# Expert blocks of two mixture-of-experts layers: sixteen uniform blocks plus three spares, or blocks by rank of expert with pairs of small ones

## The chip, the cores and the metric

One core of one Trainium2 chip runs the whole program. The metric is device time in microseconds, the median of several executions. TensorE is called PE below, VectorE DVE, ScalarE ACT, GpSimd POOL and SyncE SP; PEld is PE's loading of the stationary operand.

## The reference

The model is a first block (delta rule, dilated attention, a product-key expert layer) and two further layers. Each of these two ends in a mixture layer over T = 256 tokens, width D = 1024, with 16 experts of hidden width 512; every token picks 2 experts:

```python
weight = p_grp_sel * top_p / jnp.sum(top_p, axis=-1, keepdims=True)
expert = grp[:, None] * MOE_EXPERTS_PER_GROUP + top_i
...
def expert_block(args):
    xblk, e = args                     # 128 rows
    return (jax.nn.silu(xblk @ w1[e]) * (xblk @ w3[e])) @ w2[e]
```

So 512 rows in all are spread over 16 experts, each with w1 and w3 (1024x512) and w2 (512x1024), 2 MB each in float32: 96 MB of weights a layer. Only the two mixture layers are changed.

## The kernel before

`moe_blocks` runs one mixture layer after a normalisation stage that also makes the router's logits. DVE finds each token's two experts, PE counts how many rows each expert has, and DVE works out block and place of each row. An expert that has over 128 rows gets a second block from three spare ones, so there are NB = 19 blocks of 128 rows: sixteen by expert number, three whose expert is read from `moe_overflow_expert` at run time. POOL gathers a block's rows from DRAM (`moe_block_rows`, indirect DMA), and stores each block's result; at the end it gathers the rows back for every token, and the last two blocks are combined by PE from SBUF (`combine`).

A product of a block is made exact enough by splitting: ACT copies the weights to a rounded type (`high`, L2464), DVE subtracts that from the original (`low`, L144), and three products, low by high, high by low and high by high (L150, L151, L152), are summed in PSUM. A 2 MB weight matrix is split in two halves of 128x2048. The same is done to the block's transposed rows (ACT L2479, DVE L144) and to the hidden values (L2509, L144). A block has 8 x 3 products for w1, as many for w3 and 4 x 2 x 3 for w2: 72 products of 128x512, and 12 transposes (8 of rows, L2381; 4 of hidden values, L2390).

The weights come through a ring of three slots of 2 MB, loaded by SP: load m waits until both halves of slot m-3 are split, and does not wait for PE. `weight_parts` has room for two split matrices. As experts are taken in their own order, the plan of loads is fixed, and the stage before the mixture layer has already filled all three slots. The order on PE in block i is: w1 of i, transposes of the rows of i+1, w3 of i, w2 of i-1, transposes of the hidden values of i.

Each engine works through its instructions in the order written. A wait holds up everything that stands behind it on that engine.

Of the kernel before, what the change touches and what calls it, by code (L numbers as in the profile page):

```python
# [77 lines left out]
def shape_constants():  # L78
# [17 lines left out]
    cst[:, C_PLACE:C_PLACE + P] = p + 1  # L96
# [58 lines left out]
class WeightStream:  # L155
# [3 lines left out]
    def __init__(self, nc, ctx):  # L159
        self.ring = ctx.enter_context(nc.sbuf_tensor("weight_ring", [P, SLOTS, SLOTW], F32))  # L160
        self.loaded = [ctx.enter_context(nc.semaphore(f"weights_loaded_{i}")) for i in range(SLOTS)]
        self.used = ctx.enter_context(nc.semaphore("weights_used"))
        self.plan = []
        self.issued = 0
        self.taken = 0
# [5 lines left out]
    def add_block(self, src, k, width):  # L171

        self.plan.append((src.rearrange("p (k n) -> p k n", k=k), k, width))

    def add_later(self, k, width):

        self.plan.append((None, k, width))
# [4 lines left out]
    def load(self, sp, upto):  # L182

        for n in range(self.issued, min(upto, len(self.plan))):
# [2010 lines left out]
OVER = 3  # L2195
NB = NE + OVER


def slot_w1(i):

    return 3 * i - 1 if i else 0


def slot_w3(i):

    return 3 * i if i else 1


def slot_w2(i):

    return 3 * i + 4 if i < NB - 1 else 3 * NB - 1


def plan_moe(S, layer):

    w1, w3, w2 = (S.dram[f"moe_{n}_2"][layer] for n in ("w1", "w3", "w2"))

    def one(src, i, k, width):  # L2220
        if i < NE:
            S.w.add_block(src[i], k, width)
        else:
            S.w.add_later(k, width)
    for i in range(NB):
        one(w1, i, KD, FF)
        one(w3, i, KD, FF)
        if i:
            one(w2, i - 1, FF // P, D)
    one(w2, NB - 1, FF // P, D)  # L2230
# [14 lines left out]
def moe_blocks(S, layer, lg, p8, rows_of_x, rows_of_y):  # L2245
# [4 lines left out]
    EARLY, MIX_AT = NB - 2, 4  # L2250
    with Stage(S, "moe") as st:
# [8 lines left out]
        late = st.sb("pick_early_late", [P, 3, 2 * NT])  # L2260
        token_mix = st.sb("token_mix", [P, 4, P])
        place_mix = st.sb("place_mix", [P, 4, P])
# [7 lines left out]
        less = st.sb("expert_before", [P, NE, NE])  # L2270
        ov = st.sb("overflows", [P, NE])
        oc = st.sb("overflow_rank", [P, NE])
        wide_ov = st.sb("overflow_before", [P, NE, NE])
        at_hot = st.sb("at_pick", [P, 2 * NT, NE])
        pos = st.sb("pick_place", [P, 2 * NT])
        rank = st.sb("pick_rank", [P, 2 * NT])
        ov4 = st.sb("pick_over", [P, 2 * NT])
        blk = st.sb("pick_block", [P, 2 * NT])
        yrow = st.sb("pick_row_f", [P, 2 * NT])
        yix = st.sb("pick_row", [P, 2 * NT], U32)  # L2280
# [3 lines left out]
        ox = st.sb("overflow_hot", [P, OVER, NE])  # L2284
        oe = st.sb("overflow_expert_f", [P, OVER])
        oei = st.sb("overflow_expert", [P, OVER], U32)

        wp = st.sb("weight_parts", [P, 2, 2, SLOTW])
        xg = st.sb("block_rows", [P, 2, D])
        xt = st.sb("block_x_parts", [P, 2, 2, KD, P])  # L2290
        g = st.sb("hidden", [P, FF])
        gt = st.sb("hidden_parts", [P, 2, 2, FF // P, P])
        y = st.sb("block_out", [P, 2, D])
        xr = st.sb("first_pick_rows", [P, NT, D])
        pick_rows = (xr, S.hT[:, :, :].rearrange("p k t -> p (k t)").rearrange("p (a d) -> p a d", a=NT))
        places = st.sb("places", [P, C_ALL - C_PLACE])
        block_number = places[:, P + 4:P + 4 + NB].rearrange("p (o n) -> p o n", o=1)
        place = places[:, 0:P].rearrange("p (o n) -> p o n", o=1)
        token = places[:, P:P + 2 * NT].rearrange("p (q o) -> p q o", o=1)

        chain, shifted, exped, hot_made, counted, placed, indexed, experts_known = (st.sem(n) for n in (
            "chain", "shifted", "exped", "hot_made", "counted", "placed", "indexed", "experts_known"))
        mixed, mix_turned, mix_moved, early_gated, last_gated, combined = (st.sem(n) for n in (
            "mixes_made", "mixes_turned", "mixes_moved", "early_gated", "last_gated", "combined"))
        back_turned, back_moved, places_in = (st.sem(n) for n in ("x_turned_back", "x_rows_moved", "places_in"))
        x_stored = [st.sem(f"x_rows_stored{a}") for a in range(NT)]
        high_made, split_made, spent = (st.sem(n) for n in ("weights_high", "weights_split", "weights_spent"))
# [7 lines left out]
        n0, N = S.w.taken, 3 * NB  # L2315
        w1, w3, w2 = (S.dram[f"moe_{n}_2"][layer] for n in ("w1", "w3", "w2"))
        ident = S.cst[:, C_ID:C_ID + P]
        H1, H3, XT, GT, Y, RB = 0, 1, 2, 4, 5, 7
        BACK = (0, 1, 5, 6)
        half = lambda m, h: wp[:, m % 2, :, h * SLOTW // 2:(h + 1) * SLOTW // 2]  # L2320
        raw_half = lambda m, h: S.w.ring[:, (n0 + m) % SLOTS, h * SLOTW // 2:(h + 1) * SLOTW // 2]
# [3 lines left out]
        iota = lambda n: S.cst[:, C_IOTA:C_IOTA + n].rearrange("p (o n) -> p o n", o=1).to_broadcast([P, NT, n])  # L2325
        with nc.Block() as block:
            @block.sync
            def _(sp):
                sp.dma_start(places[:, :], S.dram["cst"][:, C_PLACE:C_ALL]).then_inc(places_in, 16)
                S.w.load(sp, n0 + SLOTS)  # L2330

                def load(m, src):

                    _, k, width = S.w.plan[n0 + m]
                    sp.wait_ge(split_made, 2 * (m - SLOTS) + 2)
                    sp.dma_start(S.w.view(n0 + m, k, width), src).then_inc(S.w.loaded[(n0 + m) % SLOTS], 16)
                for m in range(SLOTS, slot_w1(NE)):
                    load(m, S.w.plan[n0 + m][0])
# [16 lines left out]
            def _(pe):  # L2355
# [19 lines left out]
                def turn_x(i):  # L2375
                    pe.wait_ge(gathered[i % 2], 16 * (i // 2 + 1))
                    if i:
                        pe.wait_ge(xt_high, i)
                        pe.wait_ge(xt_low, i)
# [664 lines left out]
```

## Time and profile before

| | |
|---|---|
| three runs | 2562.29, 2553.57, 2560.84 us, median 2560.84 |
| span of the profiled execution | 2554.6 us |
| median less this span | 6.2 us; the record has no other time of the profiled execution |
| mean granted TensorE clock | 0.958 of full speed |
| first mixture layer, first product to last addition | 1540.28 to 1904.54 us of the span |
| second mixture layer | from about 2188 us to the end |
| weight loads of the two layers | 114 of 2 MB |

A row of the timeline gives start, duration, engine, line and operation, with its output and inputs. The profiler's matmul durations hold a fixed tail, so the distance between two starts is the cost of one in a run of them. A plain float32 matmul leaves two records, one of float32r leaves one.

### The profile page before, as it was taken

The page shows a single profiled execution, that of the slowest core. Times are in us where ns is not written, and L with a number is a line of the kernel's source. Part 1 is how long each engine was busy: PE and PEld are TensorE (multiplying, and loading weights), DVE is VectorE, ACT ScalarE, POOL GpSimd, SP SyncE. Part 2 cuts the span into 40 slices and gives each one's busy share as a digit, 9 for nine tenths or more (in the row PEclk, how much of TensorE's full clock was granted, in tenths as well). Part 3 has the DMA queues.
Part 4 walks back from the last instruction along what each step waited for, and adds up shares of the span by engine and source line. Part 5 has one row for each costly group of instructions (what it writes and reads, how often), then busy time and mean ns, then how long its engine had stood idle before and what let it go on. Part 6 is the DMA issues. An engine that isn't in the chain of part 4 may idle for free. (4 is left out here: it accounts for less than half of the span.)

```text
span 2554.6 us, 29254 instructions
## 1 busy us (share of the span) xinstructions
PE 2229.2 (87%) x11200; PEld 1600.9 (63%) x11200; DVE 1765.0 (69%) x2586; ACT 848.7 (33%) x1127; POOL 474.8 (19%) x418
## 2 busy tenths in 40 slices
PE   7788998888987777777898989999989778999998
PEld 6688886564532222222477957788869575678886
DVE  5355643458888886555654667898887575788988
ACT  1311101111111110000102325777750331677785
POOL 1032000113443434344120011000010021101001
PEclk9789999999999999999987999999999978999999
DMA  5720663439999999999562028999984504799996
GB/s 204 270 100 2 231 198 132 169 110 399 408 421 421 421 422 422 421 417 422 221 179 99 1 94 299 373 409 411 413 307 165 198 2 179 268 379 403 411 412 263
DMA packets 147335, 707.36 MB, mean 277 GB/s; under 512 B 16039, under 2 KB 20799, under 8 KB 99675
## 3 DMA queue, kind: packets, MB, share of 16 engines
q1 hardware_dynamic: 96604, 391.84, 40.2%
q0 software_dynamic: 48640, 310.47, 29.6%
q10 hardware_dynamic: 1952, 3.18, 0.4%
q8 instruction: 90, 1.47, 0.2%
q14 instruction: 49, 0.40, 0.0%
HBM read 684.40 MB, written 21.05 MB: 276 GB/s over the span
## 5 line engine op out<-in xcount | busy, mean ns | idle before, releaser
L144 DVE TENSOR_TENSOR moe_weight_parts<-weight_ring,moe_weight_parts 128x2048 fp32r<-128x2048 f32 x228 | 512.2, 2288 | 57.5 <-ACT moe_weight_parts L2464 57.2
L1608 PE MATMUL psum<-peer_uv_rows,peer_weight_diagonal 128*128 128x512 f32 x932 | 453.2, 615 | 107.5 <-DVE peer_weight_diagonal L1734 107.2
L2464 ACT ACTIVATE moe_weight_parts<-weight_ring 128x2048 fp32r<-128x2048 f32 x228 | 423.4, 1910 | 45.3 <-DMA weight_ring<-moe_w 40.7
L1608 PEld LDWEIGHTS psum<-peer_uv_rows,peer_weight_diagonal 128*128 128x128 f32 x932 | 161.9, 190 | 389.5 <-DVE peer_weight_diagonal L1734 263.3
L1741 DVE SCALAR_TENSOR_TENSOR peer_uv_rows<-peer_uv_rows,peer_x 128x1024 f32<-128x1024 f32 x233 | 285.6, 1226 | 142.5 <-DMA peer_uv_rows<-peer_uv,peer_index 140.3
L1562 POOL DMA_INDIRECT peer_uv_rows<-peer_uv,peer_index x233 | 242.2, 1040 | 385.8 <-PE psum L1608 330.6
L150 PE MATMUL psum<-moe_weight_parts,moe_block_x_parts 128*128 128x512 f32 x608 | 247.1, 406 | 7.1 <-DVE moe_weight_parts L144 5.6
L152 PE MATMUL psum<-moe_weight_parts,moe_block_x_parts 128*128 128x512 f32 x608 | 239.8, 394 | 0.0
L151 PE MATMUL psum<-moe_weight_parts,moe_block_x_parts 128*128 128x512 f32 x608 | 239.7, 394 | 0.0
L1641 ACT ACTIVATE peer_gelu<-peer_dots 128x1 f32<-128x1 f32 x256 | 51.5, 202 | 548.1 <-DVE peer_uv_rows L1741 497.1
L144 POOL TENSOR_TENSOR project_x_parts<-h_t,project_x_parts 128x1024 fp32r<-128x1024 f32 x16 | 52.7, 3312 | 533.1 <-ACT project_x_parts L630 533.1
L144 DVE TENSOR_TENSOR project_weight_parts<-weight_ring,project_weight_parts 128x2048 fp32r<-128x2048 f32 (+2 forms) x60 | 146.0, 2433 | 2.1
L150 PEld LDWEIGHTS psum<-moe_weight_parts,moe_block_x_parts 128*128 128x128 f32 x608 | 115.9, 191 | 32.5 <-issue 10.5
L152 PEld LDWEIGHTS psum<-moe_weight_parts,moe_block_x_parts 128*128 128x128 f32 x608 | 115.8, 191 | 25.5
L151 PEld LDWEIGHTS psum<-moe_weight_parts,moe_block_x_parts 128*128 128x128 f32 x608 | 116.3, 191 | 22.1
L2522 POOL DMA_DIRECT2D moe_results<-moe_block_out x34 | 19.7, 580 | 585.8 <-ACT moe_block_out L2486 585.8
L150 PE MATMUL psum<-moe_weight_parts,moe_hidden_parts 128*128 128x512 f32 x304 | 122.0, 401 | 4.5 <-DVE moe_hidden_parts L144 4.5
L150 PE MATMUL psum<-project_weight_parts,project_x_parts 128*128 128x512 f32 (+2 forms) x320 | 123.8, 387 | 0.0
L151 PE MATMUL psum<-project_weight_parts,project_x_parts 128*128 128x512 f32 (+2 forms) x320 | 122.0, 381 | 0.0
L152 PE MATMUL psum<-project_weight_parts,project_x_parts 128*128 128x512 f32 (+2 forms) x320 | 122.0, 381 | 0.0
L152 PE MATMUL psum<-moe_weight_parts,moe_hidden_parts 128*128 128x512 f32 x304 | 119.3, 392 | 0.0
L151 PE MATMUL psum<-moe_weight_parts,moe_hidden_parts 128*128 128x512 f32 x304 | 119.0, 392 | 0.0
(543 smaller groups left out, 3835.0 us busy)
## 6 DMA issues: line engine op xcount, KB each, us to landing
weight_ring<-moe_w SPq DMA_DIRECT2D x114, 2048.0 KB, 10.6
weight_ring<-ada_w SPq DMA_DIRECT2D x24, 2048.0 KB, 9.5
weight_ring<-w_in SPq DMA_DIRECT2D x17, 2048.0 KB, 8.6
moe_results<-moe_block_out POOLq DMA_DIRECT2D x34, 512.0 KB, 10.9
weight_ring<-hgrn_w_in SPq DMA_DIRECT2D x8, 2048.0 KB, 10.7
weight_ring<-nsa_w_in SPq DMA_DIRECT2D x5, 2048.0 KB, 9.1
weight_ring<-peer_wq SPq DMA_DIRECT2D x4, 2048.0 KB, 10.2
weight_ring<-w_out SPq DMA_DIRECT2D x2, 2048.0 KB, 10.4
```

Source lines behind the costliest of these rows:

```text
L144: return eng.tensor_tensor(out.bitcast(F32R), x, high, ALU.subtract)
L150: nc.tensor.matmul(out, ll, rh, start=start, stop=False)
L151: nc.tensor.matmul(out, lh, rl, start=False, stop=False)
L152: return nc.tensor.matmul(out, lh, rh, start=False, stop=stop)
L1562: nc.gpsimd.indirect_dma_start(buffer(t), None, S.dram["peer_uv"], bass.IndirectOffsetOnAxis(ap=experts[:, t:t + 1], axis=0)).then_inc(row ...
L1608: last = nc.tensor.matmul(S.ps[:, 2 * a + c, :], diag[:, t % 4, :], v_rows(t)[:, c * BANK:(c + 1) * BANK], start=(i == 0), stop=(i == PICK ...
L1641: act.activation(act_of[:, t:t + 1], dots[:, t:t + 1], ACT.Gelu_apprx_tanh).then_inc(geared, 1)
L1741: nc.vector.scalar_tensor_tensor(u_rows(t), u_rows(t), 1.0, x2[:, t // PICKS, :], ALU.mult, ALU.mult, accum_out=dots[:, t:t + 1]).then_inc ...
L2464: act.activation(half(m, h)[:, 0, :].bitcast(F32R), raw_half(m, h), ACT.Copy).then_inc(high_made, 1)
L2522: pool.dma_start(rows_of_y[i * P:(i + 1) * P, :], y[:, i % 2, :]).then_inc(y_stored[i % 2], 16)
```

## The change

Experts are ranked by how many rows they have. There are 15 blocks (jobs) in 12 units: ranks 0 to 2 have two blocks each that share one read of the weights ("doubled"), ranks 3 to 7 one block each ("single"), and ranks 8 to 15 are taken in pairs: one block holds 64 rows of one expert and 64 of the other. All weights are read once, 48 loads a layer in place of 57. A pair is not split: its products are plain float32, two for each step, one for each half of 64 columns of the stationary operand, and each writes its own 64 partitions of PSUM.

All loads now depend on the ranking, so none is issued before DVE has made it (`experts_known`), and the stage before does not load ahead (`hold`). The ring has a fourth slot. A slot of a split matrix is released when it is split, a slot of a pair only when PE has used it (`plain_spent`). The split halves have four places, as before. The first nine jobs run in three groups, each a doubled unit and a pair. Only the last job is combined from SBUF. Ranking adds some ten small DVE operations before the first gather. Core of the diff:

```diff
-OVER = 3
-NB = NE + OVER
+NB = 15
+RING = SLOTS + 1
+HALVES = 4
+    unit = [((0,), (0, 1)), ((8, 9), (11,)), ((1,), (2, 3)), ((10, 11), (12,)), ((2,), (4, 5)), ((12, 13), (13,)),
+            ((3,), (6,)), ((4,), (7,)), ((5,), (8,)), ((6,), (9,)), ((7,), (10,)), ((14, 15), (14,))]
+def phase_order():
+    for g in range(3):
+        for w in "132":
+            order += [(2 * g, w), (2 * g + 1, w)]
+    order += [(6, "1"), (6, "3")]
+    for u in range(6, LAST):
+        order += [(u + 1, "1"), (u, "2"), (u + 1, "3")]
+    return order + [(LAST, "2")]
 def plan_moe(S, layer):
+    S.w.hold()
+        def released(eng, m):
+            u, w, _ = SLOT_OF[m]
+            if PAIR[u]:
+                eng.wait_ge(plain_spent, PLAIN_AT[u, w] + 1)
+            else:
+                eng.wait_ge(split_made, 2 * SPLIT_AT[u, w] + 2)
 @@ SP @@
+                sp.wait_ge(experts_known, 1)
+                for m, (u, w, side) in enumerate(SLOT_OF):
...
+                    if m >= RING:
+                        released(sp, m - RING)
...
+                    sp.dma_start(slot(m).rearrange("p (k n) -> p k n", k=steps[w]), src).then_inc(loaded[m % RING], 16)
 @@ PE @@
+                def up_pair(u, w, first, end):
...
+                        for side in range(2):
+                            half = slice(64 * side, 64 * side + 64)
+                            last = nc.tensor.matmul(S.ps[half, LANES[2][w == "3"], :], xp[:, k, half], weights[side][:, k, :],
+                                                    start=(k == 0), stop=(k == KD - 1))
+                for gr in range(3):
...
+                    else:
+                        up(a, "1", 0)
+                    turn_x(jq, 0)
+                    up(a, "1", 1)
+                    turn_x(jq, 1)
+                    up_pair(q, "1", 0, KD)
+                    up(a, "3", 0)
+                    up(a, "3", 1)
+                    up_pair(q, "3", 0, 2)
+                    turn_x(jq + 1, 0)
+                    up_pair(q, "3", 2, 4)
+                    turn_hidden(ja)
+                    up_pair(q, "3", 4, 6)
+                    turn_x(jq + 1, 1)
+                    up_pair(q, "3", 6, KD)
+                    turn_hidden(jb)
+                    down(a, 0)
+                    turn_hidden(jq)
+                    down(a, 1)
+                    turn_x(jq + 2, 0)
+                    down_pair(q, 0, 2)
+                    turn_x(jq + 2, 1)
+                    down_pair(q, 2, 4)
+                for u in range(6, LAST - 1):
+                    up(u + 1, "1", 0)
+                    turn_hidden(i)
+                    up(u + 1, "1", 1)
+                    turn_x(i + 2, 0)
+                    down(u, 0)
+                    turn_x(i + 2, 1)
+                    down(u, 1)
+                    up(u + 1, "3", 0)
+                    up(u + 1, "3", 1)
 @@ ACT, in a group (s = 3 * gr) @@
+                    high(2 * s + 2)
+                    x_high(jq, 0)
+                    high(2 * s + 3)
+                    x_high(jq, 1)
+                    silu(ja)
+                    silu(jb)
+                    silu(jq)
+                    high(2 * s + 4)
+                    high(2 * s + 5)
+                    x_high(jq + 1, 0)
+                    hidden_high(ja)
+                    x_high(jq + 1, 1)
+                    hidden_high(jb)
+                    high(2 * s + 6)
+                    hidden_high(jq)
+                    high(2 * s + 7)
+                    out(ja)
+                    out(jb)
+                    x_high(jq + 2, 0)
+                    x_high(jq + 2, 1)
+                    out(jq)
 @@ DVE, in a group @@
+                    low(2 * s + 2)
+                    low(2 * s + 3)
+                    low(2 * s + 4)
+                    low(2 * s + 5)
+                    gate(ja)
+                    gate(jb)
+                    x_low(jq + 1, 0)
+                    hidden_low(ja)
+                    x_low(jq + 1, 1)
+                    hidden_low(jb)
+                    gate(jq)
+                    low(2 * s + 6)
+                    low(2 * s + 7)
+                    x_low(jq + 2, 0)
+                    x_low(jq + 2, 1)
```

`high(n)` waits for the load of the matrix that half n belongs to. `turn_x(i, r)` transposes half r of a job's rows and waits until ACT has taken the half before it (`xt_high`). `turn_hidden` waits for `gate`. ja, jb and jq are the two jobs of the doubled unit and that of the pair.

## Rows read from the trace of the kernel before

**Rows 1.** The page: span, and busy time of PE with its share.

```profile
span 2554.6 us, 29254 instructions
...
PE 2229.2 (87%) x11200; PEld 1600.9 (63%) x11200; DVE 1765.0 (69%) x2586; ACT 848.7 (33%) x1127; POOL 474.8 (19%) x418
```

**Rows 2.** Both mixture layers as stretches: busy by engine, clock, DMA share, GB/s.

```profile
1540.00:1897.00 357.00, 346.57 (x1594) 283.06 (x1595) 308.96 (x201) 260.48 (x188) 33.54 (x38) 0.98 0.94 376
...
2187.00:2540.00 353.00, 344.04 (x1594) 280.68 (x1594) 308.26 (x199) 261.15 (x188) 33.88 (x38) 0.99 0.94 377
```

**Rows 3.** PE's timeline in steady blocks: start, duration, operation.

```profile
1690.33 0.60 PE L2390 MATMUL psum<-constants,moe_hidden 128*128 128x128 f32 x4
...
1696.26 1.03 PE L2381 MATMUL psum<-constants,moe_block_rows 128*128 128x128 f32 x8
...
1708.19 0.60 PE L2390 MATMUL psum<-constants,moe_hidden 128*128 128x128 f32 x4
...
1800.05 0.39 PE L150 MATMUL psum<-moe_weight_parts,moe_block_x_parts 128*128 128x512 f32 x1
...
1800.96 0.39 PE L151 MATMUL psum<-moe_weight_parts,moe_block_x_parts 128*128 128x512 f32 x1
```

**Rows 4.** Groups by form, 1540 to 1897: count, busy us, mean ns, idle before.

```profile
L144 DVE TENSOR_TENSOR moe_weight_parts<-weight_ring,moe_weight_parts 128x2048 fp32r<-128x2048 f32 x112 | 251.6, 2288 | 29.2 <-ACT moe_weight_parts L2464 29.0
L2464 ACT ACTIVATE moe_weight_parts<-weight_ring 128x2048 fp32r<-128x2048 f32 x110 | 204.4, 1910 | 25.1 <-DMA weight_ring<-moe_w 22.3 <-PE psum L152 2.7
...
L2486 ACT ACTIVATE moe_block_out<-psum 128x1024 f32<-128x1024 f32 x18 | 18.5, 1028 | 28.7 <-PE psum L152 28.7
...
L144 DVE TENSOR_TENSOR moe_hidden_parts<-psum,moe_hidden_parts 128x512 fp32r<-128x512 f32 x19 | 13.1, 690 | 4.8 <-ACT moe_hidden_parts L2509 4.6
L2660 DVE TENSOR_TENSOR moe_hidden<-moe_hidden,psum 128x512 f32<-128x512 f32 x19 | 12.9, 681 | 3.2 <-PE psum L152 3.2
...
L2509 ACT ACTIVATE moe_hidden_parts<-psum 128x512 fp32r<-128x512 f32 x19 | 11.3, 592 | 2.3 <-PE psum L2390 2.3
```

**Rows 5.** PE's timeline: float32 products on four 32-column parts of the array.

```profile
87.77 1.95 PE L342 MATMUL psum<-weight_ring,cond 128*32 128x128 f32 x64
```

**Rows 6.** PE's timeline: two full float32 products of 512 columns.

```profile
802.58 1.98 PE L1608 MATMUL psum<-peer_uv_rows,peer_weight_diagonal 128*128 128x512 f32 x4 [0.50 <-DVE peer_weight_diagonal L1734]
```

**Rows 7.** Issue to landing: L2336; conditioning loads at 63.4; load at 1534.69; block gathers.

```profile
DMA to landing us min/median/max: 7.9/10.6/12.4
...
weight_ring<-ada_w SPq DMA_DIRECT2D x2, 2048.0 KB, 11.0
...
weight_ring<-moe_w SPq DMA_DIRECT2D x1, 2048.0 KB, 9.8
...
DMA to landing us min/median/max: 5.2/15.9/17.8
```

**Rows 8.** A stall of PE: timeline at 1634, and the stretch behind it.

```profile
1630.15 0.60 PE L2390 MATMUL psum<-constants,moe_hidden 128*128 128x128 f32 x4
...
1634.00 1.11 PE L2432 MATMUL psum<-constants,moe_token_mix 128*128 128x128 f32 x4 [3.26 <-DVE moe_token_mix L2643]
...
1637.00:1639.00 2.00, 2.00 (x6) 1.56 (x5) 1.35 (x1) 0.00 (x0) 0.00 (x0) 0.50 1.00 424
...
1642.68 1.04 PE L2381 MATMUL psum<-constants,moe_block_rows 128*128 128x128 f32 x8
```

**Rows 9.** Timeline at the first layer's start.

```profile
1524.59 0.18 DVE L2591 TENSOR_REDUCE moe_totals<-psum 128x16 f32<-128x32 f32 x1
...
1536.82 1.04 PE L2381 MATMUL psum<-constants,moe_block_rows 128*128 128x128 f32 x8
...
1540.28 0.47 PE L150 MATMUL psum<-moe_weight_parts,moe_block_x_parts 128*128 128x512 f32 x1 [0.70 <-issue]
```

**Rows 10.** Timeline at the first layer's end.

```profile
1896.25 7.03 PE L2422 MATMUL psum<-moe_block_out,moe_place_mix 128*128 128x512 f32 x16
...
1903.32 1.22 DVE L2704 TENSOR_TENSOR h<-h,psum 128x1024 f32<-128x1024 f32 x1 [0.42 <-PE psum L2422]
```

More of the change, by code:

```diff
@@ L163, in __init__ @@
         self.plan = []
+        self.holds = []
         self.issued = 0
@@ L182, in load @@
     def load(self, sp, upto):
-        for n in range(self.issued, min(upto, len(self.plan))):
+        for n in range(self.issued, min([upto, len(self.plan)] + self.holds[:1])):
             if n >= SLOTS:
@@ L2354, in _ @@
+                for j in range(SLOTS):
+                    m = N - RING + (j - N) % RING
+                    if m == SLOT_AT[LAST, "3", 1]:
+                        sp.wait_ge(added, NT)
+                    released(sp, m)
+                    if j == 0:
+                        S.w.holds.pop(0)
+                    S.w.load(sp, n0 + j + 1)
             @block.tensor
@@ new lines, in down_pair @@
+                def down_pair(u, first, end):
+                    i, = JOBS_OF[u]
+                    weights = raw(u, "2")
+                    pe.wait_ge(gt_high, i + 1)
+                    for f in range(first, end):
+                        for c in range(2):
+                            for side in range(2):
+                                half = slice(64 * side, 64 * side + 64)
+                                last = nc.tensor.matmul(S.ps[half, LANES[2][c], :], gp[:, f, half], weights[side][:, f, c * 512:(c + 1) * 512],
+                                                        start=(f == 0), stop=(f == FF // P - 1))
+                    if end == FF // P:
+                        last.then_inc(plain_spent, 1)
@@ new lines, in _ @@
+                up_pair(LAST, "1", 0, 4)
+                turn_hidden(LATE - 1)
+                up_pair(LAST, "1", 4, KD)
+                down(LAST - 1, 0)
+                down(LAST - 1, 1)
+                up_pair(LAST, "3", 0, KD)
+                pe.wait_ge(mixed, NT)
+                for a in range(NT):
+                    last = nc.tensor.transpose(S.ps[:, XB, a * P:(a + 1) * P], ohs[:, a, :], ident)
+                last.then_inc(mix_turned, 1)
+                turn_hidden(LATE)
+                down_pair(LAST, 0, FF // P)
@@ new lines, in _ @@
+                n = 2 * SPLIT_AT[6, "3"]
+                high(n)
+                high(n + 1)
+                high(n + 2)
+                silu(JOBS_OF[6][0])
+                high(n + 3)
+                high(n + 4)
+                high(n + 5)
+                n += 6
+                for u in range(6, LAST - 1):
+                    i, = JOBS_OF[u]
+                    hidden_high(i)
+                    for h in range(6):
+                        if n + h < 2 * len(SPLITS):
+                            high(n + h)
+                        if h == 0:
+                            x_high(i + 2, 0)
+                        if h == 1:
+                            silu(i + 1)
+                        if h == 2:
+                            x_high(i + 2, 1)
+                        if h == 3:
+                            out(i)
+                    n += 6
@@ new lines, in _ @@
+                n = 2 * SPLIT_AT[6, "3"]
+                for h in range(5):
+                    low(n + h)
+                gate(JOBS_OF[6][0])
+                low(n + 5)
+                n += 6
+                for u in range(6, LAST - 1):
+                    i, = JOBS_OF[u]
+                    hidden_low(i)
+                    for h in range(6):
+                        if n + h < 2 * len(SPLITS):
+                            low(n + h)
+                        if h == 0 and not PAIR[JOBS[i + 2][0]]:
+                            x_low(i + 2, 0)
+                        if h == 2 and not PAIR[JOBS[i + 2][0]]:
+                            x_low(i + 2, 1)
+                        if h == 4:
+                            gate(i + 1)
+                    n += 6
```

598 lines of the change are left out of this document (317 added, 281 removed).

## The prediction

> **What bounds the kernel now.** I read the page first, for the shares: PE is busy for 87% of 2554.6 us [rows 1]. That average says little of the two layers that change, so I next took them as stretches [rows 2]. PE is busy for 346.57 of 357 us and 344.04 of 353, at full clock, with the DMA engines at 0.94. Both limits are near. The timeline shows which one sets the pace: transposes of hidden values start at 1690.33 and 1708.19, a period of 17.86 us a block [rows 3]. Products follow each other by (1800.96 - 1800.05) / 4 = 0.227 us, so 72 of them are 16.3 us, and the 12 transposes take the other 1.5 us (0.13 each). PE never waits in such a block; it is the bound. The first layer runs from its first product at 1540.28 [rows 9] to its last addition, 1903.32 + 1.22 = 1904.5 [rows 10]: 364.3 us. Of this 19 x 17.87 = 339.5 are blocks and 24.8 are start, one stall and end.
>
> **The work that PE gets.** Eleven blocks stay split, 11 x 17.87. A pair has 16 + 8 steps, each of two float32 products of 512 columns on separate halves of the array. One such product at full width costs about (1.98 - 0.27) / 2 = 0.85 us, where 0.27 is the tail that a last record holds over its pitch [rows 6]. Do two halves run at once? The row that tells is the conditioning product: 64 records, which are 32 float32 products of 128 columns on four separate 32-column parts, in 1.95 us with the tail [rows 5]. One product of 128 columns is a quarter of 0.85, 0.213; 32 one after another would be 6.8 us, eight rounds of four at once are 1.7. So the parts run at once, and a pair's step costs 0.85, its 24 steps 20.5 us; one after another is the upper end, 41. On PE alone a group (two split blocks and a pair) is 6 x 5.44 + 20.5 + 36 transposes (4.7) = 57.8 us, for four blocks or 71.5 us before. That would be 13.7 won in each of three groups.
>
> The Trainium skill ("TensorE: Matmul & The Clock Gate", Measured speedup vs the span model) has 2.38 times for three column tiles, not three. At that efficiency a step would be 1.07 us by estimate, and the group 5.2 us dearer; the trace's four parts do not agree with it.
>
> **What the loads cost now.** Before, load m waited for a split, and three slots were full beforehand. Now a pair's slots come free only when PE has used them, and the ring is four deep. A group's nine loads are a1, q1, q1, a3, q3, q3, a2, q2, q2 (a the doubled unit, q the pair). Load m waits for m-4, so:
> - at the end of the pair's w1 phase the second q3 and a2 can start;
> - at the end of its w3 phase the second q2 and the next a1;
> - at the end of its w2 phase the second next q1 and the next a3.
>
> SP stands at each of these waits with all later loads behind it. The price of a restart: a lone 2 MB load lands 7.9 us after issue [rows 7]. The second adds at least 2.1 MB at the stretch's own pace: three loads and 1 MB of rows in 17.87 us is 7.34 MB, 411 GB/s, so 5.1 us. The ends for two are therefore 13.0 and, from the pair at 63.4, where the median 11.0 of both leaves 14.1 for the second and it was issued about 0.6 later, 14.7. I take 13.5, nearer to the MoE's rate. A load among gathers took 9.8 instead of 7.9 [rows 7]; rows of 0.5 MB cost 1.3 us each at that rate. At the group's end a gather and two stores are in flight, but the first microseconds of a load's latency cover most of it: 14.7 there. For the next a1 one gather counts half: 14.0.
>
> The Trainium skill ("DMA: Bandwidth & Descriptors", Anatomy of one DMA) gives 2.0 us + bytes / 436e3, by estimate 6.8 us for a lone load and 11.6 for two. By it a group would be 5.6 us shorter; the trace's minimum of 7.9 does not agree.
>
> **The chain through a group**, with ACT halves at 1.9, DVE halves at 2.29, moves of 512 columns at 0.6 on ACT and 0.69 on DVE, outputs at 1.03 [rows 4], all in written order:
> 1. From the end of the pair's w2 to a3's landing, 14.7. `high(2s+2)` 1.9, and only behind it `x_high(jq, 0)` 0.6, for which `turn_x(jq, 1)` on PE waits; 0.5 for it; then w1 of the pair, 8 x 0.85 = 6.8; 0.3 of gaps. 24.8 in all. PE had only 2 x 5.44 + 0.5 = 11.4 us of other work there and then idles about 6.
> 2. From there to a2's landing, 13.5. `high` 1.9, both `low` 4.6 (DVE has them ahead of `gate(ja)`), gate 0.7, `turn_hidden(ja)` 0.5, four pair steps 3.4, a transpose group 0.5, gaps 0.2: 11.8. Together 25.3. PE's own work up to `turn_hidden(ja)` is 10.9 + 3.4 + 0.5 after the first point; a2's chain is 20.7, so it idles some 6 us again.
> 3. From there to the next a1, 14.0. `high(2s+6)` 1.9, `hidden_high(jq)` 0.6, for which `down_pair` waits, `high(2s+7)` 1.9, two outputs 2.1, `x_high(jq+2, 0)` 0.6, the transposes 0.5, the last four steps 3.4, gaps 0.2: 11.2. Together 25.2. PE idles about 4 and then 1 us.
>
> The sum is 75.3 us, against 71.5 for the same four blocks now: loads, ACT's order and the pair make a ring of waits. The first group starts with four slots on order and takes about 73.7.
>
> **The clock.** In the stall at 1634 PE waited for 3.26 us, the granted clock was then 0.50 (1.2 GHz), and from the transposes at 1630.15 the next came at 1642.68 where 5.93 + 3.26 would have done [rows 3, 8]: 3.3 us lost, some 0.5 of it other transposes. So a stall of 3 us cost nearly its own length again. The three stalls of a group are as long or longer, and behind each stands pair work that the next loads wait for. I price each at 2.2 (ends 0 and 3.4), 6.5 a group: 81.8 us, 80 for the first.
>
> **Singles.** PE's 17.87 stays. ACT has 6 x 1.9 + 2 x 0.6 + 0.6 + 0.6 + 1.03 = 14.8 and DVE 6 x 2.29 + 4 x 0.69 = 16.5 us a block, both under it, and splits run two matrices ahead. The fourth and fifth load of this stretch start only at the last group's end, which costs about 5 us once, less what overlaps: up(6) to the end of iteration 9 is 88.4 us at full clock, 90.7 with one dip, for five blocks or 89.4 before.
>
> **Start.** `experts_known` comes seven small DVE operations (about 2.8 us) after the totals at 1524.59 [rows 9], 1527.4; with 1.5 for SP's register reads and 8 for the load, slot 0 is there at about 1537.5, split by 1541.7. The longer DVE sequence puts the first transposes 1.9 later than 1536.82. First product 1542.4, which is +2.1. The earlier stages lose nothing, they only no longer load ahead.
>
> **End.** The last pair's second w3 and both w2 loads start when its w1 is done: 7.9 + 5.2 + 5.2 + 1.2 of contention, so w2 starts 27 us after the unit does and ends at 33.9; the gathers of the results, behind `plain_spent`, land by 36 to 37, then DVE's row mixing, the gated output, the combination and the additions: 45.2 us, 48.2 with clock dips. Now the two blocks and the end cost 364.3 - 17 x 17.87 = 60.5, with the 16 us of early stalls in it.
>
> **Sum for a layer:** 2.1 + 80 + 2 x 81.8 + 90.7 + 48.2 = 384.6 against 364.3, +20.3. Two layers: +40.6 on a span of 2554.6, 2595. The median stood 6.2 above that span, so 2601 us, 1.6% slower.
>
> **The rivals.**
> - *The same waits at a lower price.* Loads of two in 13.0 us and no dip: a group is 72 and a layer 347.7 with a slightly shorter start, singles and end; -16.6 a layer, 2528 us. At 13.5 to 14.7 without a dip a layer is 2.1 + 73.7 + 150.6 + 88.4 + 45.2 = 360.0: -4.3 a layer, 2552 us, at the edge of what can be told. For it: the dip after 1634 hid partly behind other work; against: each stall here is longer. The point that decides is a group of 76 us: above it the layer loses. Chances 0.14 and 0.12.
> - *The loads don't hold anything up*, because they land before ACT needs them: PE's 57.8 a group, a layer of 303, 2439 us. For it: 48 loads and 15 blocks' rows (100.7 + 15.7 MB) are only 283 us of DMA at 411 GB/s. Against: a four-slot ring with slots freed by PE. Chance 0.12.
> - *The halves of a pair run one after another.* w1 +6.8, w3 +3.4 (the first four steps are hidden), w2 +5.5, over six groups 94 us, and about 31 in the two last units: 2726 us. [rows 5] speak against it. Chance 0.06.
> - The forecast: 0.56, its own range 2565 to 2640.
>
> **How the numbers follow.** About 0.3% (8 us) is what a measurement here tells from nothing. Faster takes the cheap waits and the unhindered loads, 0.26; same the 2552 case, 0.12; slower 0.62. The range leaves out 2439 and 2726 (0.18 together): 2520 to 2650.
>
> **What would show it.** PE idle for 4 to 6 us three times a group, before the pair's w1 (behind ACT's `x_high`), within its w3 (behind DVE's `gate`) and before its w2 (behind `hidden_high`), with ACT's `high` waiting for loads; load to landing near 8 to 14 us; a group of about 82 us; the clock at 0.5 behind the stalls; a pair's w1 phase of 6.8 us. I am wrong if the weights' landing is not what ACT waits for, if pair steps are not 0.85, or if the clock holds.

## The result, and the profile after

The changed kernel takes 2609.94 us (median of 4, from 2605.97 to 2616.59), the kernel before 2560.87 in the same comparison: a ratio of 1.0203 (95% interval 1.0182 to 1.0224), 2.0% slower. The forecast was 2601. The page and the two layers as stretches, over stretches of the same length as in [rows 1, 2] (busy us by engine, granted clock, DMA share, GB/s):

```profile
span 2608.5 us, 28034 instructions
...
PE 2174.5 (83%) x10700; PEld 1441.2 (55%) x10700; DVE 1435.0 (55%) x2420; ACT 584.6 (22%) x993; POOL 455.9 (17%) x402
```

```profile
1541.00:1898.00 357.00, 300.55 (x1288) 196.94 (x1288) 140.53 (x109) 133.59 (x121) 23.08 (x27) 0.91 0.75 302
2222.00:2575.00 353.00, 300.04 (x1290) 195.12 (x1290) 139.60 (x108) 133.16 (x121) 23.08 (x27) 0.91 0.75 303
```

DVE does less than half of what it did there, and PE's busy share, the DMA share and the clock all fell in the first layer: 0.84 for 0.97, 0.75 for 0.94, 0.91 for 0.98. With nothing near its limit, I looked for engines that wait for each other in turn. PE's timeline shows where (start, duration, operation, idle time before it and what ended it):

```profile
1545.04 1.94 PE L2433 MATMUL psum<-constants,h_t 128*128 128x128 f32 x8 [7.29 <-DMA h_t<-moe_tokens,moe_block_tokens]
...
1547.63 0.76 PE L150 MATMUL psum<-moe_weight_parts,moe_block_x_parts 128*128 128x512 f32 x1 [0.65 <-ACT moe_block_x_parts L2610]
...
1564.20 7.09 PE L2499 MATMUL psum<-weight_ring,moe_pair_x 128*64 128x512 f32 x32
...
1592.13 1.11 PE L2443 MATMUL psum<-constants,moe_hidden 128*128 128x128 f32 x4 [5.42 <-DVE moe_hidden L2772]
...
1616.39 0.79 PE L2513 MATMUL psum<-moe_weight_ring_end,moe_hidden 128*64 128x512 f32 x1 [4.93 <-ACT moe_hidden L2625]
...
1643.98 1.09 PE L2433 MATMUL psum<-constants,h_t 128*128 128x128 f32 x4 [6.47 <-issue]
...
1674.01 1.12 PE L2443 MATMUL psum<-constants,moe_hidden 128*128 128x128 f32 x4 [5.31 <-DVE moe_hidden L2772]
...
1697.44 3.41 PE L2513 MATMUL psum<-weight_ring,moe_hidden 128*64 128x512 f32 x10 [4.06 <-ACT moe_hidden L2625]
...
1723.77 1.09 PE L2433 MATMUL psum<-constants,h_t 128*128 128x128 f32 x4 [5.20 <-issue]
```

The first hidden transposes of each group (`turn_hidden(ja)`, L2443) start at 1592.13, 1674.01 and 1754.61: periods of 81.9 and 80.6 us. Each group has one stall within the pair's w3 and one ahead of its w2, and all but the first have one ahead of the pair's w1 (before `turn_x(jq, 1)`, put down to issue). What the engines that PE waits for were themselves waiting for is on ACT's timeline of two of these stalls, and on DVE's of the third:

```profile
1613.85 1.91 ACT L2596 ACTIVATE moe_weight_parts<-weight_ring 128x2048 fp32r<-128x2048 f32 x1 [13.57 <-DMA weight_ring<-moe_w]
1615.67 0.58 ACT L2625 ACTIVATE moe_hidden<-psum 128x512 f32<-128x512 f32 x1
...
1641.48 1.91 ACT L2596 ACTIVATE moe_weight_parts<-weight_ring 128x2048 fp32r<-128x2048 f32 x1 [11.46 <-DMA weight_ring<-moe_w]
1643.30 0.58 ACT L2607 ACTIVATE moe_pair_x<-psum 128x512 f32<-128x512 f32 x1
```

```profile
1668.86 4.49 DVE L144 TENSOR_TENSOR moe_weight_parts<-moe_weight_ring_end,moe_weight_parts 128x2048 fp32r<-128x2048 f32 x2 [20.86 <-ACT moe_weight_parts L2596]
1673.27 1.28 DVE L2772 TENSOR_TENSOR moe_hidden<-moe_hidden,psum 128x512 f32<-128x512 f32 x2
```

ACT stands for 11 to 14 us at a split whose load has not landed, and a move of 0.58 us that PE needs, and that could have been done, stands behind it. DVE is idle for 20.86 us, then splits for 4.49, and only then does the gates. The waits of the first layer, summed (us, times, longest), and the landing of its loads and of the page's:

```profile
ACT moe_weight_parts L2596 <- DMA weight_ring<-moe_w: 78.8, 8, 13.6
...
ACT moe_weight_parts L2596 <- DMA moe_weight_ring_end<-moe_w: 31.3, 3, 13.3
...
PE psum L2443 <- DVE moe_hidden L2772: 19.9, 5, 5.4
...
PE psum L2513 <- ACT moe_hidden L2625: 13.7, 3, 4.9
PE psum L2433 <- issue: 11.7, 2, 6.5
```

```profile
weight_ring<-moe_w SPq DMA_DIRECT2D x72, 2048.0 KB, 13.1
```

Behind two of the stalls, in which PE had been idle for 4.93 and 5.31 us, the windows show a granted clock of 0.50, the lower level (1.2 GHz):

```profile
1617.00:1620.00 3.00, 3.00 (x10) 1.17 (x8) 3.00 (x2) 3.00 (x4) 0.00 (x0) 0.50 0.08 33
...
1675.00:1677.00 2.00, 2.00 (x7) 0.72 (x8) 0.84 (x2) 0.60 (x1) 0.00 (x0) 0.50 0.04 8
```

And the end of the layer, DVE's and PE's timelines (before: [rows 10]):

```profile
1909.88 0.72 PE L2513 MATMUL psum<-weight_ring,moe_hidden 128*64 128x512 f32 x1 [2.96 <-DMA moe_weight_ring_end<-moe_w]
...
1924.89 6.57 PE L2584 MATMUL psum<-moe_block_out,moe_pair_x 128*128 128x512 f32 x8 [6.24 <-issue]
```

```profile
1916.49 0.75 DVE L2923 TENSOR_SCALAR weight_ring<-weight_ring,moe_pick_late_early 128x1024 f32<-128x1024 f32 x1 [10.28 <-DMA weight_ring<-moe_results,moe_pick_row]
...
1923.57 1.22 DVE L2937 TENSOR_TENSOR moe_block_out<-psum,ada_gate 128x1024 f32<-128x1024 f32 x1
...
1931.50 1.22 DVE L2944 TENSOR_TENSOR h<-h,psum 128x1024 f32<-128x1024 f32 x1 [1.59 <-PE psum L2584]
```

The last pair's w2 is done at 1918.66 (the timeline's last L2513 record), but DVE has begun with two rows of mixing at 1916.49, and the gated output that PE's combination needs comes after them.

### The profile page after: what moved, and what is told of

It is laid out like the page before. It is cut to its first block and busy times, and to the rows that moved or that the text cites. A ratio compares the mean times of both kernels' runs of the same rounds, so it can differ in the third digit from the quotient of the medians.

```text
span 2608.5 us, 28034 instructions
## 1 busy us (share of the span) xinstructions
PE 2174.5 (83%) x10700; PEld 1441.2 (55%) x10700; DVE 1435.0 (55%) x2420; ACT 584.6 (22%) x993; POOL 455.9 (17%) x402
## 5 line engine op out<-in xcount | busy, mean ns | idle before, releaser
L144 DVE TENSOR_TENSOR moe_weight_parts<-weight_ring,moe_weight_parts 128x2048 fp32r<-128x2048 f32 x68 | 155.2, 2291 | 267.1 <-ACT moe_weight_parts L2596 266.9
L2596 ACT ACTIVATE moe_weight_parts<-weight_ring 128x2048 fp32r<-128x2048 f32 x68 | 129.0, 1909 | 187.1 <-DMA weight_ring<-moe_w 180.7
L150 PE MATMUL psum<-moe_weight_parts,moe_block_x_parts 128*128 128x512 f32 x352 | 144.7, 411 | 8.0 <-DVE moe_weight_parts L144 6.7
L2715 POOL DMA_INDIRECT h_t<-moe_tokens,moe_block_tokens x30 | 34.4, 1148 | 636.3 <-PE psum L2433 545.6
L151 PE MATMUL psum<-moe_weight_parts,moe_block_x_parts 128*128 128x512 f32 x352 | 140.9, 400 | 0.0
L152 PE MATMUL psum<-moe_weight_parts,moe_block_x_parts 128*128 128x512 f32 x352 | 140.4, 399 | 0.0
L2499 PE MATMUL psum<-weight_ring,moe_pair_x 128*64 128x512 f32 x416 | 135.1, 666 | 6.1 <-DMA weight_ring<-moe_w 6.1
L144 DVE TENSOR_TENSOR moe_weight_parts<-moe_weight_ring_end,moe_weight_parts 128x2048 fp32r<-128x2048 f32 x28 | 64.0, 2291 | 87.8 <-ACT moe_weight_parts L2596 87.7
L139 DVE CAST project_weight_parts<-weight_ring 128x2048 fp32r<-128x2048 f32 (+2 forms) x60 | 86.5, 1442 | 37.2 <-PEq L571 30.1
L150 PE MATMUL psum<-project_x_parts,project_weight_parts 128*128 128x256 f32 x320 | 91.1, 285 | 0.0
L1731 DVE TENSOR_SCALAR peer_weight_diagonal<-constants,peer_gelu,peer_gates 128x128 f32<-128x128 f32 x256 | 87.9, 344 | 5.2 <-ACT peer_gelu L1638 5.2
L152 PE MATMUL psum<-project_x_parts,project_weight_parts 128*128 128x256 f32 x320 | 90.6, 283 | 0.0
## 6 DMA issues: line engine op xcount, KB each, us to landing
weight_ring<-moe_w SPq DMA_DIRECT2D x72, 2048.0 KB, 13.1
```

The source lines that it names most:

```text
L139: return nc.vector.tensor_copy(out.bitcast(F32R), x)
L144: return eng.tensor_tensor(out.bitcast(F32R), x, high, ALU.subtract)
L150: nc.tensor.matmul(out, ll, rh, start=start, stop=False)
L151: nc.tensor.matmul(out, lh, rl, start=False, stop=False)
L152: return nc.tensor.matmul(out, lh, rh, start=False, stop=stop)
L1731: nc.vector.tensor_scalar(diag[:, t % 4, :], S.cst[:, C_ID:C_ID + P], act_of[:, t:t + 1], gates[:, t:t + 1], ALU.mult, ALU.mult).then_inc( ...
```

## The experiments

The question was what the stalls consist of: the price of the loads (a ring of four slots freed by PE), the written order on ACT and DVE in front of them, or the clock behind them. The first three runs and the fifth to seventh change the kernel after in one thing each, the others put such changes together; each ratio is to the kernel before.

**First run: ACT moves the pair's rows ahead of the splits.**

```diff
-                    high(2 * s + 2)
                     x_high(jq, 0)
-                    high(2 * s + 3)
                     x_high(jq, 1)
+                    high(2 * s + 2)
+                    high(2 * s + 3)
```

> The changed kernel with one swap on ScalarE in each group: both x_high of the pair stand ahead of high(2s+2) and high(2s+3). Theory A (a ring of waits: ScalarE's order ties the pair's rows to the landing of a3): the idle of TensorE ahead of the pair's w1 (5.2 to 6.5 us in the second and third group) goes, and with it the slow clock behind it; the pair's w1 ends about 7 us earlier, its slots are freed earlier, and the group falls from 81 to 73-75 us. The first group gains less (1.5 us). Two layers: 30 us less, 2580 (2565 to 2595). Rival B (the loads themselves or the pair's products set the pace, the order is harmless): the wait moves to the next load, 2605 to 2612. Rival C (only the late start costs): no change, 2605 to 2612.

Measured: 2587.75 us, 1.0119 (1.0087 to 1.0150), in the range. The stall ahead of the pair's w1 is gone and the other two stay; hidden transposes of two groups:

```profile
1593.32 1.12 PE L2443 MATMUL psum<-constants,moe_hidden 128*128 128x128 f32 x4 [5.22 <-DVE moe_hidden L2772]
...
1667.48 1.11 PE L2443 MATMUL psum<-constants,moe_hidden 128*128 128x128 f32 x4 [5.06 <-DVE moe_hidden L2772]
```

The period is 74.2, 7.7 less. The next one is 75.7, 4.9 less: together somewhat less than expected.

**Second run: DVE gates the hidden values ahead of the splits.**

```diff
-                    low(2 * s + 4)
-                    low(2 * s + 5)
                     gate(ja)
                     gate(jb)
+                    low(2 * s + 4)
+                    low(2 * s + 5)
                     x_low(jq + 1, 0)
```

> The changed kernel with one swap on VectorE in each group: gate(ja) and gate(jb) stand ahead of low(2s+4) and low(2s+5). Theory A: the 5 us stall within the pair's w3 nearly goes (about 1 is left, behind x_high(jq+1, 0), which still stands behind both high), the pair's w3 ends 5 to 7 us earlier and the next a1 with it; six groups: 36 us less, 2574 (2560 to 2592). Rivals B and C: 2605 to 2612.

Measured: 2587.77 us, 1.0119 (1.0089 to 1.0148), in the range but near its dear end: 22 us less than the kernel after, where 36 were expected. The stall at the hidden transposes is gone, and one half as long (about 1 us was expected) stands behind it, at `turn_x(jq + 1, 1)`, whose bank is free only after `x_low`, still behind the two splits:

```profile
1588.08 0.63 PE L2433 MATMUL psum<-constants,h_t 128*128 128x128 f32 x4 [2.75 <-DVE moe_block_x_parts L144]
```

**Third run: ACT does the pair's hidden values and the outputs, and both engines the next rows, ahead of the next group's splits.**

```diff
-                    high(2 * s + 6)
                     hidden_high(jq)
-                    high(2 * s + 7)
                     out(ja)
                     out(jb)
                     x_high(jq + 2, 0)
+                    high(2 * s + 6)
+                    high(2 * s + 7)
                     x_high(jq + 2, 1)
...
                     gate(jq)
+                    x_low(jq + 2, 0)
                     low(2 * s + 6)
                     low(2 * s + 7)
-                    x_low(jq + 2, 0)
                     x_low(jq + 2, 1)
```

> The changed kernel with the third swap alone: hidden_high(jq), the two outputs and x_high(jq+2, 0) on ScalarE stand ahead of high(2s+6), and x_low(jq+2, 0) on VectorE ahead of low(2s+6). Theory A: the stall of 4 to 5 us ahead of the pair's w2 goes, the w2 phase ends 5 to 7 us earlier; the next a3 is issued then: six groups, 36 us less, 2574 (2560 to 2592). Rivals B and C: 2605 to 2612.

Measured: 2583.7 us, 1.0103 (1.0075 to 1.0130), again in the range and a smaller gain than expected (26 us for 36). The stall ahead of w2 is gone, and the next one, ahead of the pair's w1, has grown from 6.47 to 8.39 us; PE reaches it earlier, and the load that ends it is not that much earlier. And where the singles begin, PE waits once for 10.27 us (at 1787.99) in place of 2.58 and 3.59. The larger stall ahead of w1:

```profile
1638.13 1.09 PE L2433 MATMUL psum<-constants,h_t 128*128 128x128 f32 x4 [8.39 <-issue]
```

**Fourth run: all three, and the same rule in the middle of the group.** In the group's middle, where the three runs above left splits ahead of moves, the order becomes (DVE's to match, its `low(2 * s + 5)` behind `gate(jq)`):

```diff
-                    high(2 * s + 4)
-                    high(2 * s + 5)
                     x_high(jq + 1, 0)
                     hidden_high(ja)
+                    high(2 * s + 4)
                     x_high(jq + 1, 1)
                     hidden_high(jb)
+                    high(2 * s + 5)
                     hidden_high(jq)
```

> All three swaps, and in the middle of the group both engines take the hidden values ahead of the split of a2. Theory A: TensorE has no wait of over 1 us in a group, the group is TensorE's own 58 to 62 us where it is 81 now, the granted clock stays full; six groups less the first ones' late start: 115 us less than the changed kernel, 2495 (2475 to 2525), below the kernel before. Rival B: the ring of four slots frees loads too late whatever the order; the group is 72 or more, 2555 to 2600. Rival C (start): 2605 to 2612.

Measured: 2498.23 us, 0.9775 (0.9752 to 0.9799): 2.2% faster than the kernel before and, by the two ratios, 4.2% faster than the one after, with the same loads, the same ring, the same products, and inside the expected range. The hidden transposes come 60.5 and 60.3 us apart, with no wait in front of them, and from 1600 to 1680 (second view) the stretch is full:

```profile
1583.27 0.66 PE L2443 MATMUL psum<-constants,moe_hidden 128*128 128x128 f32 x4
...
1643.78 0.66 PE L2443 MATMUL psum<-constants,moe_hidden 128*128 128x128 f32 x4
```

```profile
1600.00:1680.00 80.00, 79.26 (x368) 49.04 (x367) 25.21 (x19) 28.87 (x29) 8.63 (x9) 1.00 0.92 369
```

A ring of four slots can feed PE through the groups. The loads land no sooner (a median of 13.3 us for 13.1), but ACT waits for them for 15.9 us from its second split of the layer on, where it was 110.1. What slowed PE was that every load's slot came free late, because PE stood behind moves that stood behind the load before.

**Fifth run: the clock alone.** The kernel after, with products of constants into a bank that is free at that point, in front of each of the three stalls (in the first group, of its two); PE is kept at work while it waits, and no other instruction moves.

```diff
+                    if gr:
+                        idle_products(S, GT, 5)
                     turn_x(jq, 1)
...
+                    idle_products(S, GT, 5)
                     turn_hidden(ja)
...
+                    idle_products(S, LANES[2][0], 4)
                     down_pair(q, 0, 2)
```

> The changed kernel, orders as they are, with TensorE given products that nobody reads in the three waits of each group: 5 ahead of turn_x(jq, 1) (not in the first group), 5 ahead of turn_hidden(ja), 4 ahead of the pair's w2, each 0.85 us and so shorter than the wait. If the slow clock behind each wait is a cost of its own (2.2 us each by the prediction, 6.5 a group), the products of the pair behind the waits come at 0.43 between records again, the group falls from 81 to 75-76, and six groups save 33 us: 2577 (2565 to 2590). If the clock is hidden by the loads, or does not follow the idle time, 2605 to 2612.

Measured: 2589.15 us, 1.0113 (1.0085 to 1.0141). The same stretch in the kernel after and in this one:

```profile
1600.00:1680.00 80.00, 63.30 (x269) 37.66 (x269) 19.05 (x15) 20.05 (x21) 4.51 (x6) 0.89 0.69 274
```

```profile
1600.00:1680.00 80.00, 74.01 (x317) 43.72 (x316) 19.49 (x15) 20.36 (x21) 5.34 (x6) 1.00 0.72 284
```

The clock is whole (1.00 for 0.89), the DMA share is hardly higher, and the time falls by 0.9%, some 21 to 23 us, in the range. Behind each filling PE still waits, for 0.43 to 2.56 us in the three groups, so the added products hold nothing up. The periods are 78.1 and 76.8 us, 3.8 less each. So the clock takes 3.8 us of a group, 1.3 a stall, where I had priced 6.5 and 2.2. That is net of what comes back as a wait: at the full clock PE gets to `turn_x(jq + 2, 1)` before DVE has freed its bank.

```profile
1606.71 0.61 PE L2513 MATMUL psum<-moe_weight_ring_end,moe_hidden 128*64 128x512 f32 x1 [1.24 <-ACT moe_hidden L2629]
...
1611.55 0.63 PE L2433 MATMUL psum<-constants,h_t 128*128 128x128 f32 x4 [1.19 <-DVE moe_block_x_parts L144]
```

**Sixth run: the rows of the first two blocks ahead of the other loads.** SP issues the first load and then waits for `gathered[1]`, the rows of the second block.

```diff
+                    if m == 0:
+                        sp.wait_ge(gathered[1], 16)
```

> The changed kernel, but SyncE issues only the first weight load at once and the next three when the second block's rows have landed. If the four loads in flight are what makes the first gather slow (rows reach TensorE at 1545 where 1538.7 was forecast), the first transposes come 5 to 6 us earlier, and, as the fourth slot's landing moves little, each layer saves about 5: 2600 (2593 to 2604). If the gather is slow for another reason, the later loads cost: 2610 to 2625.

Measured: 2619.93 us, 1.0233 (1.0203 to 1.0263), a miss. By the time alone that is the second case, and the trace says otherwise. SP's loads in the kernel after and in this one, and this one's first transposes on PE, which wait for the gathered rows:

```profile
1528.90 2.99 SPq L2392 DMA_DIRECT2D weight_ring<-moe_w  x3
```

```profile
1530.18 0.36 SPq L2392 DMA_DIRECT2D weight_ring<-moe_w  x1
...
1543.11 1.48 SPq L2392 DMA_DIRECT2D weight_ring<-moe_w  x2
```

```profile
1540.88 1.07 PE L2435 MATMUL psum<-constants,h_t 128*128 128x128 f32 x8 [2.05 <-DMA h_t<-moe_tokens,moe_block_tokens]
```

That is 10.7 us behind the first load, where it was 16.1 (1528.90 to 1545.04): four loads in flight did hold the gathers up, by 5.4 us. But the three other loads are issued from 1543.11, 12.9 us after the first where it was 1.5. The fourth is a3's, and with the order of the kernel after, ACT's move of the pair's rows stands behind its split: the first group now has the stall ahead of the pair's w1 that only the others had. ACT's and PE's timelines:

```profile
1565.01 1.91 ACT L2598 ACTIVATE moe_weight_parts<-moe_weight_ring_end 128x2048 fp32r<-128x2048 f32 x1 [12.35 <-DMA moe_weight_ring_end<-moe_w]
```

```profile
1567.51 1.09 PE L2435 MATMUL psum<-constants,h_t 128*128 128x128 f32 x4 [5.43 <-issue]
```

The hidden transposes are 68.3 us behind the first load, where they were 63.2: the 5.4 us are given back about twice over. I had expected the fourth slot's landing to move little, and that was wrong.

**Seventh run: a ring of three slots.** `RING = SLOTS` in place of `SLOTS + 1`.

> The changed kernel with a ring of three slots for four. By the ring of waits each of the three restarts of a group then brings three loads ahead of the one that ScalarE waits for, 5.2 us more each, 15 a group: 2700 (2680 to 2715). If the weights' landing is not what the group waits for, 2605 to 2620.

Measured: 2737.1 us, 1.0691 (1.0666 to 1.0716), a miss: 37 us over the forecast. Two of the hidden transposes and a stall between them:

```profile
1598.71 1.11 PE L2443 MATMUL psum<-constants,moe_hidden 128*128 128x128 f32 x4 [5.88 <-DVE moe_hidden L2772]
...
1627.64 1.12 PE L2513 MATMUL psum<-weight_ring,moe_hidden 128*64 128x512 f32 x2 [10.15 <-ACT moe_hidden L2625]
...
1696.52 1.11 PE L2443 MATMUL psum<-constants,moe_hidden 128*128 128x128 f32 x4 [7.46 <-DVE moe_hidden L2772]
```

The periods are 97.8 and 99.0 us, 15.9 and 18.4 more than with four slots. From first product to the end of the third group the first layer takes 285.9 us for 241.8, 44.1 more where 45 were expected. The miss lies behind it, in what the forecast had left alone: from there to the last addition it takes 160.6 for 143.3 (a stall of 6.83 us at 1941.77, ahead of hidden transposes, is new). A load lands sooner than with four slots, after 10.6 us in the median, and yet ACT waits longer for loads: 180.6 us from its second split of the layer on, for 110.1. It is when a load may start that sets the time here, more than how long it takes.

**Eighth run: the orders of the fourth, the start of the sixth, and at the end the gated output ahead of the mixing.**

```diff
-                mix_rows(0)
-                add_rows(0)
-                mix_rows(1)
                 spent_by(dve, (LAST, "2"))
...
+                mix_rows(0)
+                add_rows(0)
+                mix_rows(1)
                 add_rows(1)
```

> The orders of the kernel that ran at 2498, with the start of the gathers-first kernel, and at the end VectorE's gated output of the last job ahead of the mixing of rows, so that TensorE's combination (which waited 6.2 us) overlaps it. Start 5 us and end 2 to 4 us a layer: 2483 (2474 to 2492). If the start's delay lies elsewhere, 2490 to 2500.

Measured: 2489.72 us, 0.9728 (0.9708 to 0.9748), in the range.

**Ninth and tenth run: its start alone, and its end alone, on the fourth's orders.**

> All six orders of the fourth run, and SP issues the first load, then waits until the first block's rows have landed, and then issues the other three; the end of the layer as changed. In the run that had this and the new end together, the first hidden transposes of the doubled unit came 53.8 us after the first load was issued, against 57.8 us with the orders alone, so 4 us a layer is the whole that the start can give: 2490 us, from 2484 to 2497. If the later start of the three other loads is given back inside the first group (as it was with the changed kernel's own order), it is 2498 or above.

> All six orders of the fourth run, and at the layer's end DVE does the gated output of the last pair ahead of the two rows of mixing; the start as changed. If PE's combination of the last pair waits for the gated output alone, the mixing of 2 x 2.0 us and an addition of 2.4 us move behind it and are done while PE works: 2 to 4 us a layer, 2492 us, from 2488 to 2496. If the final additions wait for the mixed rows in any case, nothing: 2496 to 2500 us.

Measured: with the start 2488.13 us, 0.9733 (0.9710 to 0.9756), as expected; with the end 2497.06, 0.9757 (0.9741 to 0.9773), which is over the range and in the case in which the new end gives nothing. (The wait of the ninth run, too, is for the second block's rows.) The trace with both, at the start:

```profile
1524.65 14.03 SPq L2392 DMA_DIRECT2D weight_ring<-moe_w  x3
...
1534.97 1.07 PE L2435 MATMUL psum<-constants,h_t 128*128 128x128 f32 x8 [1.56 <-DMA h_t<-moe_tokens,moe_block_tokens]
...
1578.44 0.66 PE L2445 MATMUL psum<-constants,moe_hidden 128*128 128x128 f32 x4
```

The first transposes come 10.3 us behind the first load, for 15.7 with the orders alone, and so repeat what the sixth run shows. The hidden transposes are 53.8 us behind it, against 57.8 with the orders alone (1525.44 to 1583.27). The delay of SP that cost the kernel after 5 us is a gain of 4 us here: the two moves of the pair's rows stand ahead of a3's split, ACT waits 1.57 us for its load (12.35 in the sixth run), and PE has no wait of over 2.60 us up to the hidden transposes. From first load to last addition a layer takes 345.6 us in the fourth run, 343.3 with the new start, 344.5 with the new end and 341.2 with both. The new end gives about 1. PE's combination does start earlier, 1.42 us behind the end of w2 for 6.23, but DVE has the same work in either order, and the additions, which had waited for PE, now follow DVE's own mixing without a gap. What it gives is below what these times can tell, and whether the eighth version is faster than the ninth isn't settled.

## Why the prediction was right, by its steps

The direction and the mechanism were right. That the time came so near, 2601 for 2609.94, is in part luck: two terms of the group were off by 2 to 3 us each, one up and one down, and what the start and the end had too low was partly made up by the step from span to median.

- **The group.** 81.8 us was forecast; the second and the third of the first layer, from the end of one pair's w2 to the next (1625.91, 1706.96, 1789.39 on the timeline), take 81.05 and 82.43. The first takes 78.3 for 80. The stalls stand where they were put, behind `x_high`, `gate` and `hidden_high`, and the fourth run shows that the order is the cause: with the same loads the period is 60.4.
- **But two terms of it were off, and hid each other.** The clock was 3.8 and not 6.5. The chain without it was 75.3, and the fifth run has 77.5. Landings are a part of this, and a small one: a3's split starts 15.6 us after the pair's w2 has ended (1625.91 to 1641.48), for 14.7; the three restarts of that group add up to 43.2 us for 42.2, those of the next to 42.4. Where the rest of the 2.2 us lies I did not find.
- **PE's own work in a group** was put at 57.8; the fourth run, in which PE is busy for 79.26 of 80 us, has 60.4. No run parts these 2.6 us.
- **Pair steps.** 32 records in 7.09 us with the tail of the last, [rows 5] read rightly: two halves at once, the next two records 0.43 us behind, 0.85 a step. Behind a stall the same phase takes 8.1 (1644.99 to 1653.1), as its first records are 0.85 apart at the lower clock.
- **Start.** +2.1 was the forecast; the first product is at 1547.63 and not at 1542.4. This is the term that failed most, by about 5 us a layer. I had counted the longer DVE sequence and not that the four loads, issued in one go from 1528.90, are ahead of the first rows on the DMA engines; the sixth run puts 5.4 us on it. The prediction charged loads for gathers in their way, and no gather for loads.
- **Singles and end.** 90.7 + 48.2 = 138.9 was forecast from the last group's end to the last addition; it took 143.3 (1789.39 to 1932.72). Singles have the period of 17.81 that was expected; the entry costs two waits (2.58 and 3.59 us) and comes to 92.1 for 90.7. The end is 51.2 for 48.2: w2 runs at the lower clock behind its wait (33.9 forecast from the unit's start, 37.2 measured), the gated output stands behind the mixing, and PE takes 6.57 us for eight combination products. They run at a granted clock of 0.50 behind a wait of 6.24 us; in the tenth run, behind one of 1.42, the same eight take 3.67 at 1.00.
- **The sum.** From the first product's time before (1540.28) to the last addition a layer took 392.4 us for 384.6 (0.3 of the difference lies ahead of the layer), and the span is 53.9 us longer for 40.6. The median stood 1.4 us above this span, where I had carried over the 6.2 of before; that took back 4.8 of it.
- **The rivals.** That the loads hold nothing up (2439 us) was refuted for this kernel: ACT waits 110 us a layer for them. But its size was not absurd, for with another order of ACT and DVE the same loads give 2498. Halves one after another: refuted by the pair's records. The same waits at a lower price: the fifth run comes nearest to that case, 78.1 and 76.8 us a group, and it is still 1.1% slower. The point of 76 us, below which a layer was to gain, was too high: the first run has 74.2 and 75.7 in its groups and a time still 1.2% above before. The start and the end take what the group gives. With these two as measured (a first product 7.0 us later, counted from DVE's totals, and 143.3 us behind the groups) and a first group 3.4 below the average, my estimate of the point is (364.3 - 7.0 - 143.3 + 3.4) / 3, about 72.5 us.

By the formula of the Trainium skill ("DMA: Bandwidth & Descriptors", Anatomy of one DMA), which the page gives for transfers that GpSimd issues, a restart of two loads was 11.6 us by estimate, and the group 5.6 us shorter. Here SyncE issues them, and in this trace the eight restarts of the first layer's groups take 13.5 to 15.6 us until ACT's split begins; they do not agree with it.

What stays open: the three single orders give 0.8, 0.8 and 1.0% over the kernel after, and the fourth run 4.2%. It holds more than the three (the middle of the group), and I ran nothing that parts what this middle gives from what the three give together.

## What to carry to other kernels

When a ring of buffers is freed by the last engine in line, each engine on the way should do everything that needs no new buffer ahead of what waits for one. In this kernel that was a reordering of ACT and DVE alone, worth 4.2% (a ratio of 1.0203 became 0.9775), where a slot taken away cost 4.8% and the clock 0.9%. Mend such waits together and judge them together: one at a time they gave 0.8 to 1.0% each, and part of the time that one gave came back in the next stall (6.47 us grew to 8.39). A change that looks bad alone (SP holding its loads back, +5 us a layer up to the first hidden transposes) may be good once the order is right (-4 us).

## What was not expected of the hardware

- The 2 MB loads of a ring of four land after 13.1 us (median of the 72 into `weight_ring`), those of a ring of three after 10.6: each load is quicker then, and the kernel 4.8% slower. In the fourth run they land after 13.3, no sooner than in the kernel after, and it is 4.2% faster.
- With four 2 MB loads issued ahead of the first gathers of 0.5 MB, PE's first transposes come 5.4 us later than with one.
- Products of constants in front of the stalls hold the granted clock at 1.00 where it was 0.89 in the same stretch, and are worth 21 to 23 us in all, in a kernel that is limited by waits.
